# Columns of the streamed products in pieces of four, alternating between the two halves of a block

## The reference

```python
# first block
u = _rmsnorm(h, norm_w)
proj = jnp.matmul(u, w_in.astype(jnp.float32))
...
y_a = jnp.matmul(h_a, w_out[:ML_WIDTH])
y_b = jnp.matmul(h_b, w_out[ML_WIDTH:])
...
# second block, two layers
h = x @ w_in
mkv = mem @ w_mem_kv
out = y @ w_out
return layer_norm(DEEPNORM_ALPHA * x + out, ln_g, ln_b)
```

## Time and profile before

| | us |
|---|---|
| median of 2 runs | 2179.88 |
| lowest and highest | 2177.82 and 2181.93 |
| span of the profiled execution | 2177.5 |
| TensorE busy in it | 2149.8 |
| VectorE busy | 1279.1 |
| ScalarE busy | 1110.0 |

### The profile page before, as it was taken

One profiled execution on the slowest core, in us unless ns is written; L12 is line 12 of the kernel. 1 busy time (PEld: TensorE's weight loads), 2 busy tenths in 40 slices (PEclk: granted clock), 3 DMA queues, 4 the chain that ended last, 5 costly groups with the idle time before them and its releaser, 6 DMA issues.

```text
span 2177.5 us, 32782 instructions
## 1 busy us (share of the span) xinstructions
PE 2149.8 (99%) x12468; PEld 1773.4 (81%) x12468; DVE 1279.1 (59%) x1505; ACT 1110.0 (51%) x1480; POOL 127.7 (6%) x205
## 2 busy tenths in 40 slices
PE   8999999999999999999999999999999999999998
PEld 7888888888888777777878888888888788888886
DVE  6455546464545757575765564566546845566467
ACT  6554545454435748374655554455544544545343
POOL 6000000000000100001010000000000210000002
PEclk9999999999999999999999999999999999999999
DMA  9766565566565544454546766745567566554644
GB/s 345 250 184 192 175 195 177 184 202 193 193 194 174 156 146 145 123 176 129 167 138 199 241 195 181 204 149 167 158 203 254 193 202 170 172 167 148 201 160 159
DMA packets 208227, 400.64 MB, mean 184 GB/s; under 512 B 13297, under 2 KB 30210, under 8 KB 207711
## 3 DMA queue, kind: packets, MB, share of 16 engines
q1 hardware_dynamic: 199440, 369.94, 54.8%
q0 software_dynamic: 6352, 20.49, 3.1%
q10 hardware_dynamic: 2304, 8.39, 1.1%
HBM read 389.94 MB, written 8.82 MB: 183 GB/s over the span
## 4 chain that ended last, share of the span: by engine, by line
PE 89%; ACT 3%; issue 3%; DVE 3%; DMA 1%; DVEq 0%; SPq 0%; ACTq 0%
PE stream_psum L624 26%; PE stream_psum L626 26%; PE stream_psum L625 26%; PE heads_psum L594 2%; ACT w_high L1065 1%; DVE w_low L1486 1%; PE heads_psum L797 1%; DVE work L1649 1%; ACT work L1065 1%; PE heads_psum L982 1%; PE heads_psum L944 1%; PE heads_psum L925 1%; PE heads_psum L816 1%; DMA w_raw<-in_w_mem_kv 1%; DMA w_raw<-in_w_in 1%
## 5 line engine op out<-in xcount | busy, mean ns | idle before, releaser
L1486 DVE TENSOR_TENSOR w_low<-w_raw,w_high 128x1024 fp32r<-128x1024 f32 x688 | 830.7, 1225 | 636.9 <-ACT w_high L1065 635.7
L1065 ACT ACTIVATE w_high<-w_raw 128x1024 fp32r<-128x1024 f32 x688 | 712.6, 1058 | 457.7 <-PE stream_psum L626 399.5
L624 PE MATMUL stream_psum<-w_high,x_high 128*128 128x512 f32 x1856 | 741.9, 400 | 0.2 <-DVE w_low L1486 0.2
L626 PE MATMUL stream_psum<-w_high,x_low 128*128 128x512 f32 x1856 | 723.8, 390 | 0.2 <-issue 0.2
L625 PE MATMUL stream_psum<-w_low,x_high 128*128 128x512 f32 x1856 | 723.3, 390 | 0.0
L626 PEld LDWEIGHTS stream_psum<-w_high,x_low 128*128 128x128 f32 x1856 | 348.4, 188 | 74.3 <-issue 0.7
L624 PEld LDWEIGHTS stream_psum<-w_high,x_high 128*128 128x128 f32 x1856 | 348.7, 188 | 73.6 <-issue 2.5
L625 PEld LDWEIGHTS stream_psum<-w_low,x_high 128*128 128x128 f32 x1856 | 348.9, 188 | 69.2 <-issue 1.9
L624 PE MATMUL stream_psum<-w_high,y_high 128*128 128x512 f32 x896 | 353.0, 394 | 4.7 <-DVE w_low L1486 3.4
L626 PE MATMUL stream_psum<-w_high,y_low 128*128 128x512 f32 x896 | 349.0, 390 | 0.0
L625 PE MATMUL stream_psum<-w_low,y_high 128*128 128x512 f32 x896 | 348.8, 389 | 0.0
(11 more groups left out here) (300 smaller groups left out, 1245.2 us busy)
## 6 DMA issues: line engine op xcount, KB each, us to landing
w_raw<-in_w_in SPq DMA_DIRECT2D x528, 512.0 KB, 4.4
w_raw<-in_w_out SPq DMA_DIRECT2D x128, 512.0 KB, 5.0
w_raw<-in_w_mem_kv SPq DMA_DIRECT2D x32, 512.0 KB, 5.7
work<-rows_scratch POOLq DMA_DIRECT2D x8, 512.0 KB, 4.8
proj<-in_mem_t SPq DMA_DIRECT2D x8, 256.0 KB, 6.7
work<-in_x_t SPq DMA_DIRECT2D x4, 512.0 KB, 6.8
residual<-in_x SPq DMA_DIRECT2D x2, 1024.0 KB, 11.8
mkv_scratch<-proj POOLq DMA_DIRECT2D x4, 512.0 KB, 3.6
```

The lines of the kernel that those rows point to most:

```text
L624: pe.matmul(acc, hi[:, k, sl(m)], w, start=first, stop=False)
L626: return pe.matmul(acc, lo[:, k, sl(m)], w, start=False, stop=final)
L1065: return act.activation(dst, src, func, **kw)
L1486: tt(WL[:, c % RING, :], RAW[:, c % RING, :], WH[:, c % RING, :].bitcast(F32), ALU.subtract).then_inc(lo_done, 1)
```

## The change

The moving operand and the result of every stream matmul are seen through another address pattern. The 512 columns of the block are split in two halves of 256 (`two`) and each half in 64 runs (`n`) of 4 columns (`e`). The matmul takes them in the order `n two e`: columns 0 to 3, then 256 to 259, then 4 to 7, then 260 to 263, and so on. The same re-ordering is applied to the operand in `WH` or `WL` and to the result in `SP_`, so each column's result lands where it did. The fp32 values of a run of four are 16 bytes, and the jump between the halves is 1,024 bytes.

```diff
                     def passes(c, kk, m, b=b):
                         i, k = b * per + c, tiles[c] + kk
                         first, final = (c, kk) == (0, 0), (c, kk) == (per - 1, CH - 1)
-                        w, wl = WH[:, i % RING, sl(kk, NBLK)], WL[:, i % RING, sl(kk, NBLK)]
-                        acc = SP_[:, 2 * ((b + base) % 2) + m, :]
+                        two = lambda ap: ap.rearrange("p (two n e) -> p n two e", two=2, e=4)
+                        w, wl = two(WH[:, i % RING, sl(kk, NBLK)]), two(WL[:, i % RING, sl(kk, NBLK)])
+                        acc = two(SP_[:, 2 * ((b + base) % 2) + m, :])
                         pe.matmul(acc, hi[:, k, sl(m)], w, start=first, stop=False)
                         pe.matmul(acc, hi[:, k, sl(m)], wl, start=False, stop=False)
                         return pe.matmul(acc, lo[:, k, sl(m)], w, start=False, stop=final)
```

## The result

| | before | after |
|---|---|---|
| median of 2 runs, us | 2179.88 | 2354.31 |
| lowest and highest | 2177.82 and 2181.93 | 2353.74 and 2354.88 |
| span of the profiled execution | 2177.5 | 2352.1 |

The kernel became slower by 174.4 us, a ratio of 1.0792 with a 95% interval of 1.0775 to 1.081.

The account below looks back on a forecast made before the run. TensorE's stream of products was taken to bound the kernel: 1871 us of products, 0 for fetch, landing and fixed cost, and 307 us of other work gave 2178, forecast as 2180 us; range 2170 to 2725.

Parts of the forecast that it names:

- the small fixed cost: A small fixed price on each stream product for the longer address pattern, slower than the forecast; chance 0.01.
- the rival's upper bound: 2725 us, from a price for every jump in the operand fetch at 66 ns a product; that rival had 0.16.
- What bounds the kernel: TensorE's stream products in `passes`: 8256 at 226.6 ns, 1871 of 2177.5 us, with the ring of weights full.
- The 8.26 us: Kernel time claimed for each nanosecond added to a stream product of 512 columns, over 8256 products.
- Step (a), the fetch: TensorE's fetch of columns from `WH` and `WL`: claimed to pay 0 for the jumps between pieces.
- The other reading: Each non-unit step of the operand fetch has a price: 29 to 66 ns a product, 2419 to 2725 us; chance 0.16.
- the strided load: Weight load for transposes of `RES` in `feature_tiles`, taking every second value: median 208 ns against 142 for contiguous ones.
- Step (b), the landing: Writing of the products' results into `SP_` in PSUM: claimed to pay 0 for the jumps.
- The rival that put the landing at 3810 us: Jumping PSUM writes run at the fp32 pace, 424 ns a product, +1630 us; chance 0.13, including fetch and landing together.
- Step (c), a fixed cost of the pattern: A fixed price on each stream product for the longer address pattern: claimed 0, decisive from 5.3 ns a product.
- The gain: Address order was costing up to 13.3 ns a stream product; at most -110 us, 2070 us; chance 0.04.
- The signs named for the profile: Product spacing 226 to 227 ns if unchanged, 255 to 293 for fetch, near 424 for PSUM; loads and head products unmoved.

Follow-up runs that it names:

- e1_operand: The kernel after, with only the moving operand in pieces of four and the result written contiguously to PSUM; 2354.53 us.
- e4_both2: The kernel after, with operand and result in pieces of two columns in place of four; 3034.20 us.
- e2_psum: The kernel after, with only the result in pieces of four and the operand read contiguously; 2180.15 us.

## Why the prediction was right or wrong

The measured 2354.31 us lie inside the range of 2170 to 2725, on the side to which I had given 0.30. The likeliest case, no change with 0.66, is wrong. That the time lies inside is in part luck: apart from the small fixed cost at 0.01, no case gave a time between 2190 and 2419 us, and the range covers this gap only because it was drawn on to the rival's upper bound.

**What bounds the kernel** held. The stream's products are nearly the whole path, and a nanosecond on each is worth nearly what was said (174.6 us for 23.3 ns is 7.5 us for each). The 8.26 us were 10% high. "With nothing beside it that could hide it" left out TensorE's own 27.7 us of idle time, of which 10.3 came back. The rest of the difference is that TensorE's busy time grew by 22.4 ns for each of the 8256 products (184.9 us) and not by 23.3.

**Step (a), the fetch, failed.** I read the earlier trace rows as a price for the memory passed over, and took 0. e1_operand shows 23.3 ns for an operand that passes over nothing it doesn't use. The ground given for 0, pieces on whole multiples of 16 bytes and used to the last value, is no protection. The other reading, 127 steps at the price of the strided load, gave 29 to 66 ns. The place was right, but the measured price is a fifth below the lower bound, and the kernel is faster than the rival's 2419 to 2725 us.

That lower bound was itself misread from the earlier trace rows. The 154 and 125 ns are averages over all distances of a series, and the first of them is long in both series, because the first load runs beside a stream product and the second starts only when that product gives way to the first transpose, 0.23 us later. Narrower windows on the same two series in before take in only the first two loads:

```profile
1277.37 0.43 PEld L594 LDWEIGHTS heads_psum<-ident,residual 128*128 128x128 f32 x2
...
153.50 0.37 PEld L594 LDWEIGHTS heads_psum<-ident,proj 128*128 128x128 f32 x2
```

From there the strided loads take (670 - 430) / 2 = 120 ns each and the others (1020 - 370) / 6 = 108 ns. So a strided load costs some 12 ns where loads follow one another, not 29. With 12 as the lower bound the rival would have run from 2180 + 8256 x 0.012 = 2279 us to 2725, and both the 23.3 ns and the 2354 us would have been inside it.

Nor is it a price per step: 3 jumps cost 0, 15 cost 10.3 ns, 127 cost 23.3 or 6.7 by where the pieces lie. The strided load showed that TensorE's fetch isn't indifferent to order, and this should have moved the forecast; as a size it served only as a bound.

The first place where the Trainium skill was weighed, 16-byte lines with at least two hits on each, spoke for 0. The Trainium skill ("Advanced Engine Details and Errata", SBUF Cachelines) is not borne out in that strong form: pieces of four use up their lines and pay 23.3 ns (e1_operand), and pieces of two have two hits on a line and pay 106.7, there with the result in pieces of two as well (e4_both2).

**Step (b), the landing, held.** e2_psum has 226.7 ns. The rival that put the landing at 3810 us is dead for pieces of four. Of the two sentences of the Trainium skill on PSUM ("Advanced Engine Details and Errata", PSUM Cachelines) the first, that any non-contiguous pattern slows matmuls significantly, does not hold for pieces of 16 bytes: 2180.15 us beside 2181.58. The second, that pairs should stay together, agrees with it but has not been put to the test alone.

**Step (c), a fixed cost of the pattern, held** at 0: pieces of 128 have 226.7 ns and 2177.69 us. **The gain** of up to 110 us did not show in any run.

**The signs named for the profile** did their work. The transposes' loads and the head products stood still, all three lines grew alike, both waits grew, and a distance of 250 ns pointed to the fetch (255 to 293) and not to PSUM (424), though it fell just short of the span that I had named, by the misread lower bound.

What stays open is the mechanism inside the fetch: why pieces 256 or 1,024 bytes apart cost 6.7 ns more than pieces 1,008 bytes apart and slow ScalarE too, why the jumps from 3 to 15 are dearer than the later ones, and whether the load of the next tile has a part in it.

## What to carry to other kernels

In a kernel that TensorE bounds, keep the moving operand contiguous over long runs, 128 fp32 columns or more, and do the re-ordering in the result: the write to PSUM took pieces of four at no cost. When a profile offers only one row of a strided access, take it as proof that order matters on that engine and let it weigh on the forecast, but don't scale its price by the number of steps. Take such a price from distances inside an unbroken series, without the first one, which can be a wait for something else. And when an edit slows the bound engine, take off what that engine's own waits can give back.

## What was not expected of the hardware

- With the same 127 jumps an fp32r operand of 512 columns read in pieces of 16 bytes costs 16.7 ns a product at 1,008 bytes between the two runs of pieces and 23.3 ns at 256 or 1,024 bytes. Neighbours swapped, in operand and result, cost 6.7 ns.
- With pieces of four at 256 and 1,024 bytes ScalarE's writing of `WH` takes 1100 ns in place of 1058; at 1,008 bytes it takes 1056.
- Pieces of 8 bytes in operand and result cost 106.7 ns a product, a cliff after 23.3 ns for pieces of 16 bytes: 3034.20 us for the kernel.
- A stationary operand of 64 in place of 128 columns in one of three products made the stream slower, 229.7 for 226.7 ns and 2200.69 for 2178.37 us.
